# Compressed attention as products on a block diagonal, with the second half's inputs loaded into main attention

## What is computed

```python
def nsa_attend(q, q_pos, kc, vc, ...):
    dist_c = q_pos[:, None] - (jnp.arange(n_cmp) * CMP_STRIDE + (CMP_LEN - 1))[None, :]
    s_c = jnp.einsum('bqghd,bngd->bghqn', q, kc) * SCALE
    s_c = s_c + rb[rel_bucket(dist_c)].transpose(2, 3, 0, 1)
    p_c = masked_softmax(s_c, dist_c >= 0)
    o_c = jnp.einsum('bghqn,bngd->bqghd', p_c, vc)
    ...
    o = gates[:, :, 0][..., None] * o_c + gates[:, :, 1][..., None] * o_s + gates[:, :, 2][..., None] * o_w
```

## Time and profile before

| what | us |
|---|---|
| median of 3 runs | 2063.82 |
| range of the runs | 2063.62 to 2071.12 |
| profiled execution, its own time | 2058.45 |
| span of that execution | 2056.7 |
| TensorE busy | 1857.6 |
| VectorE busy | 1006.2 |
| ScalarE busy | 733.1 |
| GpSimd busy | 542.6 |

### The profile page before, as it was taken

How to read it: one execution, slowest core, us unless ns; L and a number is a source line. 1 busy time by engine, 2 the same in 40 slices (tenths; PEclk the granted TensorE clock), 3 DMA queues, 4 the chain that set the end, 5 groups by cost and what they waited for, 6 DMA issues and landing times. The chain is left out here.

```text
span 2056.7 us, 31665 instructions
## 1 busy us (share of the span) xinstructions
PE 1857.6 (90%) x11624; PEld 1628.5 (79%) x11624; DVE 1006.2 (49%) x1899; ACT 733.1 (36%) x1456; POOL 542.6 (26%) x626
## 2 busy tenths in 40 slices
PE   2988999998877889999998798999999999799995
PEld 2888877997644778778777686999999999776674
DVE  2323421333333557777777652333323232466997
ACT  2223411212322157777777431211111111133352
POOL 4310022421453422222211201112211221143452
PEclk9899999999998579999999899999999999899998
DMA  6452343356987943322221122111111111164533
GB/s 148 87 113 108 133 157 122 115 165 204 315 260 231 229 135 75 66 62 62 63 51 58 75 82 71 42 41 46 55 42 41 43 55 54 37 217 141 189 130 134
DMA packets 168965, 229.21 MB, mean 111 GB/s; under 512 B 44716, under 2 KB 113125, under 8 KB 168711
## 3 DMA queue, kind: packets, MB, share of 16 engines
q1 hardware_dynamic: 144282, 154.58, 25.0%
q0 software_dynamic: 24560, 73.03, 12.8%
HBM read 192.59 MB, written 40.18 MB: 113 GB/s over the span
## 5 line engine op out<-in xcount | busy, mean ns | idle before, releaser
L121 PE MATMUL gate_acc<-o_T_hi,w_gate_split_hi 128*128 128x352 f32 x528 | 171.6, 325 | 2.3 <-ACTq L2696 2.3
L121 PE MATMUL up_acc<-o_T_hi,w_up_split_hi 128*128 128x352 f32 x528 | 170.4, 323 | 0.7 <-DVEq L2739 0.7
L122 PE MATMUL gate_acc<-o_T_lo,w_gate_split_hi 128*128 128x352 f32 x528 | 170.3, 323 | 0.0
L123 PE MATMUL gate_acc<-o_T_hi,w_gate_split_lo 128*128 128x352 f32 x528 | 170.2, 322 | 0.0
L122 PE MATMUL up_acc<-o_T_lo,w_up_split_hi 128*128 128x352 f32 x528 | 169.2, 321 | 0.0
L123 PE MATMUL up_acc<-o_T_hi,w_up_split_lo 128*128 128x352 f32 x528 | 169.1, 320 | 0.0
L2324 DVE TENSOR_TENSOR pa_probs_T_lo<-pa_t,pa_probs_T_hi 128x512 fp32r<-128x512 f32 (+3 forms) x288 | 145.6, 528 | 38.6 <-ACT pa_probs_T_hi L2253 37.3
L2177 PE MATMUL pa_t<-ident,pa_scores 128*128 128x128 f32 x816 | 138.5, 275 | 24.8 <-DVE pa_probs_T_lo L2324 23.9
L2253 ACT ACTIVATE pa_probs_T_hi<-pa_t 128x512 fp32r<-128x512 f32 (+3 forms) x288 | 130.9, 473 | 80.1 <-PE pa_t L2177 74.5
L2238 ACT ACTIVATE pa_scores<-pa_scores,pa_neg_max 128x128 f32<-128x128 f32 (+1 forms) x192 | 143.5, 747 | 16.2 <-DVE pa_neg_max L2276 12.6
L121 PE MATMUL y_acc<-w_down_split_hi,act_split_hi 128*128 128x512 f32 x308 | 125.4, 407 | 19.0 <-DVE act_split_lo L3061 19.0
(11 more groups left out here) (441 smaller groups left out, 4765.5 us busy)
## 6 DMA issues: line engine op xcount, KB each, us to landing
w_down_raw<-in_w_down SPq DMA_DIRECT2D x59, 512.0 KB, 4.3
fox_k_pages<-in_cache_fox_kv SPq DMA_DIRECT2D x64, 256.0 KB, 6.3
w_rows<-in_cache_fox_kv POOLq DMA_DIRECT2D x48, 256.0 KB, 8.1
w_gate<-in_w_gu SPq DMA_DIRECT2D x22, 512.0 KB, 3.7
w_up<-in_w_gu SPq DMA_DIRECT2D x22, 512.0 KB, 3.7
w_rows<-in_w_in SPq DMA_DIRECT2D x5, 2048.0 KB, 10.5
sel_pages<-in_cache_nsa_kv POOLq DMA_DIRECT2D x64, 128.0 KB, 7.5
pa_k_fox<-scratch_kf_d POOLq DMA_DIRECT2D x32, 256.0 KB, 6.3
```

The source lines that it names most:

```text
L121: pe.matmul(out, a[0][at], b[0][bt], start=start, stop=False)
L122: pe.matmul(out, a[0][at], b[1][bt], start=False, stop=False)
L123: return pe.matmul(out, a[1][at], b[0][bt], start=False, stop=stop)
```

## The change

`compressed_attention` computes both key groups in one product. `kc_p` becomes 128 by 128 with each group's 63 keys on the diagonal and zeros elsewhere, and `vc_p` 128 by 136 likewise, with a column of ones for each group, so that the sum of the exponentials comes out of the value product. A tile is 4 score products, 4 turns and 4 value products, each over 128 rows. The turned probabilities are double-buffered in PSUM. VectorE's sum over the exponentials goes; the mask is multiplied into the gates once. `front` zeroes the two tiles on POOL, and `sample_attention` fills them with four copies in place of two.

POOL issues the first half's 16 loads before its fills, splits the fox values of the first half, then issues the second half's 16. SP issues the first half's six loads (the group values go straight into the upper half of the tile that they are split in), waits until the first half's keys have landed, and issues the second half's six. The other five splits are POOL's first work in main attention after its fills. SP's 4 MB copy in main attention waits until the first job is scored. The queries are loaded in two halves of the positions.

```diff
@@ front
-            pool.wait_ge(s_id, 9)
+            pool.memset(c.kc_p[:, :], 0.0).then_inc(s_id, 1)
+            pool.memset(c.vc_p[:, :], 0.0).then_inc(s_id, 1)
+            pool.wait_ge(s_id, 11)
+            for g in range(G):
+                pool.memset(c.vc_p[g * HD:g * HD + NC, P + g:P + g + 1], 1.0).then_inc(s_id, 1)
+            pool.wait_ge(s_id, 13)
@@ sample_attention, SP
-            for g in range(G):
-                sp.dma_start(c.ca_q[g * HD:(g + 1) * HD, :, :], d["qn_d"][g * GH:(g + 1) * GH, :, :].rearrange("h e n -> e h n")).then_inc(c.s_cq, 16)
+            for half in range(2):
+                cols = slice(half * T // 2, (half + 1) * T // 2)
+                for g in range(G):
+                    sp.dma_start(c.ca_q[g * HD:(g + 1) * HD, :, cols],
+                                 d["qn_d"][g * GH:(g + 1) * GH, :, cols].rearrange("h e n -> e h n")).then_inc(c.s_cq[half], 16)
@@ sample_attention, VectorE
-            dve.tensor_copy(c.kc_p[:, :], M[:, 0:NC])
-            dve.tensor_copy(c.vc_p[:, :], M[0:NC, HD:HD + P]).then_inc(s_pv, 1)
+            for g in range(G):
+                rows, cols = slice(g * HD, g * HD + NC), slice(g * HD, (g + 1) * HD)
+                dve.tensor_copy(c.kc_p[cols, rows], M[cols, 0:NC])
+                ins = dve.tensor_copy(c.vc_p[rows, cols], M[rows, HD:2 * HD])
+            ins.then_inc(s_pv, 1)
@@ compressed_attention, SP
             for u in range(2):
+                if u:
+                    sp.wait_ge(pa.s_kl[0], 16 * 8)
+                    settled(sp, c)
                 pa.load_fox_bias(sp, d, GH * u, u)
                 pa.load_fox_values(sp, d, GH * u, u)
-            for n, (kind, u) in enumerate(group):
-                if n >= 2:
-                    sp.wait_ge(pa.s_gs, n - 1)
-                src = d["nsa_kv_p"][0, 0, :, 3, u, :] if kind == "sel" else d["vw_d"][:, u * HD:(u + 1) * HD]
-                sp.dma_start(g_raw[n % 2][:, :, :], src.rearrange("(t p) e -> p t e", p=P)).then_inc(pa.s_gv[n], 16)
-            for u in range(2):
                 pa.load_nsa_bias(sp, d, GH * u, u)
+                for n, (kind, w_) in enumerate(group):
+                    if w_ == u:
+                        src = d["nsa_kv_p"][0, 0, :, 3, u, :] if kind == "sel" else d["vw_d"][:, u * HD:(u + 1) * HD]
+                        sp.dma_start(pa.low_half(kind, u), src.rearrange("(t p) e -> p t e", p=P)).then_inc(pa.s_gv[n], 16)
@@ compressed_attention, POOL (load(u) issues the 16 loads of half u)
+            load(0)
             for u in range(2):
...
-                pool.wait_ge(pa.s_fv[u], 16)
-                pa.split_values(pool, pa.v["fox"][u], pa.v_raw[u], pa.s_vs[u], u + 1)
-            for n, (kind, u) in enumerate(group):
-                pool.wait_ge(pa.s_gv[n], 16)
-                pa.split_values(pool, pa.v[kind][u], g_raw[n % 2], pa.s_gs, n + 3)
+            pool.wait_ge(pa.s_fv[0], 16)
+            pa.split_values(pool, pa.v["fox"][0], pa.v_raw[0], pa.s_vs[0], 1)
+            load(1)
@@ compressed_attention, TensorE: scores, turn, values
                 for m in range(GH):
-                    for g in range(G):
-                        rows = slice(g * HD, (g + 1) * HD)
-                        ins = pe.matmul(S[t % 2][:, g, m * NC:(m + 1) * NC], q[rows, m, t * P:(t + 1) * P], c.kc_p[rows, :],
-                                        start=True, stop=True)
+                    ins = pe.matmul(S[t % 2][:, m, :], q[:, m, t * P:(t + 1) * P], c.kc_p[:, :], start=True, stop=True)
...
-                for h in range(H):
-                    ins = pe.transpose(T_[0:NC, h, :], sc[t % 2][:, h, :], c.ident[:, :])
+                for m in range(GH):
+                    ins = pe.transpose(T_[t % 2][:, m, :], sc[t % 2][:, G * m:G * m + G, :].rearrange("p g n -> p (g n)"), c.ident[:, :])
...
-                for h in range(H):
-                    g = h // GH
-                    ins = pe.matmul(O[t % 2][:, h, :], pT[t % 2][:, h, :], c.vc_p[:, g * HD:(g + 1) * HD], start=True, stop=True)
+                for m in range(GH):
+                    ins = pe.matmul(O[t % 2][:, m, 0:P + G], pT[t % 2][:, m, :], c.vc_p[:, 0:P + G], start=True, stop=True)
@@ compressed_attention, VectorE
-            def coefficients(t):
-                cf = co[:, t, :]
-                dve.wait_ge(s_e, t + 1)
-                chain(dve.tensor_reduce(cf, sc[t % 2][:, :, :], AX, ALU.add))
...
             def output(t):
-                dve.wait_ge(s_co, t + 1)
+                cf = co[:, t, :].rearrange("p (m g) -> p m g", g=G)
                 dve.wait_ge(s_o, t + 1)
+                chain(dve.reciprocal(cf, O[t % 2][:, :, P:P + G]))
+                chain(dve.tensor_tensor(cf, cf, by_pair(gs[:, t, :]), ALU.mult))
@@ prompt_attention, SP
+            sp.wait_ge(s_s, NT + 1)
+            settled(sp, c)
             sp.dma_start(d["win_kv_s"][0, :, 0:WIN - NQ], d["state_win_kv"][0, :, NQ:WIN]).then_inc(s_wc, 16)
@@ prompt_attention, POOL, after its fills
+            for n, (kind, u) in enumerate((kind, u) for u in range(2) for kind in ("sel", "win")):
+                pool.wait_ge(pa.s_gv[n], 16)
+                pa.split_values(pool, v[kind][u], pa.low_half(kind, u), pa.s_gs, n + 2)
+            pool.wait_ge(pa.s_fv[1], 16)
+            pa.split_values(pool, v["fox"][1], pa.v_raw[1], pa.s_vs[1], 6)
@@ prompt_attention, TensorE, values of a sel job
-                        pe.wait_ge(pa.s_gs, 4)
+                        pe.wait_ge(pa.s_gs, 2 * u + 2)
```

More of the change, by code:

```diff
@@ L1765, in __init__ @@
         self.k = {kind: [[ph.sb(f"pa_k_{kind}{u}{w_}", [P, T], FR) for w_ in range(2)] for u in range(2)] for kind in kinds}
+        at_v = ph.nc.sbuf_base
         self.v = {kind: [ph.sb(f"pa_v_{kind}{u}", [P, NT, 2, HD], FR) for u in range(2)] for kind in kinds}
+        assert ph.nc.sbuf_base == at_v + 6 * 2 * NT * HD * 4
+        self.raw = {kind: [ph.nc.alloc_sbuf_tensor_at(f"pa_v_{kind}_raw{u}", [P, NT, 2, HD], F32, offset=at_v + (2 * n + u) * 2 * NT * HD * 4)
+                           for u in range(2)] for n, kind in enumerate(kinds) if n}
         self.v_raw = [ph.sb(f"pa_v_raw{u}", [P, NT, HD]) for u in range(2)]
@@ L1818, in compressed_attention @@
         q = c.ca_q
-        sc = [ph.sb(f"ca_scores{i}", [P, H, NC]) for i in range(2)]
-        pT = [ph.sb(f"ca_probs_T{i}", [NC, H, P]) for i in range(2)]
-        g_raw = [ph.sb(f"pa_group_v_raw{n}", [P, NT, HD]) for n in range(2)]
+        sc = [ph.sb(f"ca_scores{i}", [P, H, HD]) for i in range(2)]
+        pT = [ph.sb(f"ca_probs_T{i}", [P, GH, P]) for i in range(2)]
         mx = ph.sb("ca_max", [P, 2, H])
+        gs = ph.sb("ca_gates", [P, NT, H])
         co = ph.sb("ca_coef", [P, NT, H])
-        S = [ph.ps(f"ca_s{i}", [P, G, 512]) for i in range(2)]
-        T_ = ph.ps("ca_t", [P, H, P])
-        O = [ph.ps(f"ca_o{i}", [P, H, HD]) for i in range(2)]
+        S = [ph.ps(f"ca_s{i}", [P, GH, P]) for i in range(2)]
+        T_ = [ph.ps(f"ca_t{i}", [P, GH, P]) for i in range(2)]
+        O = [ph.ps(f"ca_o{i}", [P, GH, 256]) for i in range(2)]
         s_s = ph.sem("ca_scored")
+        s_z = ph.sem("ca_cleared")
         s_sh = ph.sem("ca_shifted")
@@ L1856, in _, with load @@
         def _(pool):
[L1857 to L1861, removed]
+            def load(u):
                 pa.load_fox(pool, d, GH * u, u)
@@ L1867, in _ @@
                             pool.dma_start(pa.k[kind][u][w_][r * HD:(r + 1) * HD, :], d[src][w_, u]).then_inc(pa.s_kl[u], 16)
+            load(0)
             for u in range(2):
-                pool.wait_ge(pa.s_fv[u], 16)
-                pa.split_values(pool, pa.v["fox"][u], pa.v_raw[u], pa.s_vs[u], u + 1)
-            for n, (kind, u) in enumerate(group):
-                pool.wait_ge(pa.s_gv[n], 16)
-                pa.split_values(pool, pa.v[kind][u], g_raw[n % 2], pa.s_gs, n + 3)
+                pool.memset(pa.bias["sel"][u][:, 0:T - 256], 0.0).then_inc(pa.s_bz, 1)
+                pool.memset(pa.bias["win"][u][:, P:WIN + P - 256], 0.0)
+                pool.tensor_copy(pa.bias["win"][u][:, 0:P], misc(c, "wmask", P)).then_inc(pa.s_bz, 1)
+            pool.wait_ge(pa.s_fv[0], 16)
+            pa.split_values(pool, pa.v["fox"][0], pa.v_raw[0], pa.s_vs[0], 1)
+            load(1)
         @block.tensor
@@ L1877, in scores @@
             def scores(t):
[L1878 to L1879 removed]
+                if t % (NT // 2) == 0:
+                    pe.wait_ge(c.s_cq[t // (NT // 2)], 16 * G)
                 if t >= 2:
@@ L1930, in _ @@
             chain = Chain(dve, s_ch)
-            chain.enter(0, NT * 5)
+            chain.enter(0, 3 + NT * 4)
             lo = MISC["seen"][0]
+            by_pair = lambda y: y.rearrange("p (g m) -> p m g", g=G)
+            chain(dve.tensor_tensor(gs[:, :, :], c.gates[:, 0:NT, 0:H], c.misc[:, lo:lo + NT * H].rearrange("p (t h) -> p t h", h=H), ALU.mult))
+            for x in sc:
+                chain(dve.memset(x[:, :, NC:HD], 0.0))
             def shifted(t):
```

(10 more changed lines are left out.)

36 lines of the change are left out of this document (15 added, 21 removed).

## The result

The changed kernel takes 2055.13 us (median of 5 runs, 2051.48 to 2060.25); the kernel before, run beside it, took 2063.82 (2060.8 to 2072.01). The ratio is 0.995 with a 95% interval of 0.9926 to 0.9973: faster by 6 to 15 us, where 18.4 were forecast, and outside the range of 2032 to 2052. The profiled execution took 2058.64 us, its span is 2056.9.

The account below looks back on a forecast made before the run. TensorE at the lower clock was taken to bound compressed attention, SP's held issues to end it after the change. 18.7 us saved less 0.3 for copies gave 18.4: 2045.4 us from the 2063.82 median, range 2032 to 2052.

Parts of the forecast that it names:

- Rival (d): Compressed attention, TensorE: wide f32 passes don't overlap weight loads, 0.44 us each, 14 us slower, 2078 us; chance 5%.
- The rule on weight loads: TensorE: a weight load overlaps a running matmul only when the row group differs, true of nothing after the change.
- The queries in halves and the small fills: Ahead of the stage: about 1.7 us more on SP and 1 us on POOL, both expected to hide in waits.
- (a): Compressed attention: SP isn't held by a full queue, computation ends the stage; 2032 us, or 2044 at lower clock; chance 18%.
- (c): Main attention gives the gain back through late POOL merges or second-half values, 10 us or more; 2054 to 2064; chance 9%.
- Rival (b): Compressed attention ends later, at 724 to 730, by 0.26 us passes or a slower queue; 2047 to 2054 us; chance 8%.
- the sum of the part on the transfers: Compressed attention: SP's last issue ends at 720.8, main attention starts at 721.5 in place of 740.26, 18.7 us less.
- The rate of POOL's packets: Compressed attention: POOL's and SP's queues move 69 packets a us each, one for one; POOL's is through at 718.4.
- The end of the block: End of compressed attention: main attention starts 0.74 us after SP's last issue, the last of the engines' work.
- The room in SP's queue: Compressed attention: SP's queue holds 2300 to 2600 packets, so its last issue ends with 4310 to 4610 of 6912 done.

Follow-up runs that it names:

- the transfers alone: The kernel before with only the change's transfers and value splits, the old narrow products kept: 2065.21 us, ratio 0.9997 to the kernel before.

## Why the prediction was wrong

**Right.** TensorE bound the stage at the lower clock and does so no longer; the wide passes cost 0.235 and 0.11 us; the upper clock came, and the computation ended 29.6 us after the start against 30.8 forecast. Rival (d) is out: a pass of 0.235 us, not 0.44. The rule on weight loads that the prediction names beside it, from the Trainium skill ("TensorE: Matmul & The Clock Gate", Part 3, The mechanism), does not hold for these passes. The stage ends on transfers with TensorE idle, and an issue of SP of many us stands before it. POOL's splits and the delayed copy, both moved behind the stage, cost nothing that shows: the rest after the stage is 1316.7 against 1316.4. The queries in halves and the small fills lie ahead of a stage whose start varies by 13 us, so these profiles can't show their microsecond. Rivals (a) and (c) are out as well. Rival (b), to which I gave 8%, is what happened: it had a slower queue and the stage's end at 724 to 730, and 677.2 + 50.2 is 727.4. Its 2047 to 2054 still ends 1 us under the median of the result.

**The step that failed** is the sum of the part on the transfers, which took SP's last issue plus 0.74 us for the end of the stage. The stage ended on another path, POOL's packets and the DRAIN behind them, and these packets were slower than forecast. The sum let main attention start 44.3 us after the stage did; it was 50.2. All its counts can be held against the DMA queues of the changed kernel (windows 694.15 to 702, 702 to 715.2, and 715.2 to 737.1, then SP's from the start to 731.6, to 735.8 and to 737.5; packets, MB, share):

```profile
q0 software_dynamic: 368, 1.24, 74.8%
q1 hardware_dynamic: 1117, 0.48, 51.9%
...
q0 software_dynamic: 947, 3.10, 95.3%
...
q0 software_dynamic: 1243, 4.04, 78.5%
q1 hardware_dynamic: 2426, 1.22, 53.3%
...
q1 hardware_dynamic: 3601, 1.79, 45.7%
...
q1 hardware_dynamic: 4249, 2.24, 48.2%
...
q1 hardware_dynamic: 5231, 2.65, 50.7%
```

1. *The rate of POOL's packets* is the term that made the time. I took 69 a us, from the middle of the stage before, for the whole of it, and one packet of SP for one of POOL's. It was 368/7.85 = 47 in the first 8 us, where SP's queue moved three packets for one of POOL's, 947/13.2 = 72 then, and 1243/21.9 = 57 for the second half, with a slow tail: 236 packets in the last 6.8 us, beside 1252 of SP's. POOL's queue was through 46.7 us after the start, not 41.2. The earlier start of POOL, on which I counted, bought little: its 1280th packet began 24.7 us after the start of the stage in the changed kernel and 25.3 in the kernel before, whose first had come 2.8 us later.
2. *The end of the block.* I took 0.74 us behind SP's last issue, which is right when VectorE or SP is last, and never asked for POOL beyond its last issue. POOL's packets ended at 736.79, its DRAIN at 739.16, and main attention began at 740.24, 3.45 us behind the packets. SP alone (737.50 and 1.0) would have given 738.5.
3. *The room in SP's queue.* I had 2300 to 2600 packets from two issues. Each of SP's loads also has 16 packets of 4 B, which I had left out: 3552 a half and 7104 in all, not 3456 and 6912. The long issue was let go when 3601 of the 4736 packets issued before it had begun (3593 in the kernel without the wait), so with about 1130 left; SP's last issue ended with 5231 of 7104 begun, so with 1870 left. SP's queue had begun 4249 by 735.8, and would by the forecast's room have let SP go just behind, at about 736; it went on to 737.50. So SP was free 47.5 us after the start, not 43.6. By itself this set nothing, since POOL's DRAIN ended 1.4 us after SP's.

The account of the 5.9 us is then: POOL's packets were through 5.5 us later than forecast, and the way from there to main attention (3.45 us) is 0.35 longer than the 3.1 that the forecast had from POOL's last packet, by way of SP, to the same point. It was luck that the missing wait was so small a term: by the forecast's own rate POOL's queue ends at 41.2, and with 3.45 main attention begins at 44.6, beside the 44.3 of the sum. As a mechanism it is what the prediction lacked. It holds the stage at 44.6 us when SP has no second half to issue, and of the 19 us between the changed kernel's stage and that of the best version, 17.6 go when POOL's second half alone goes, 5.6 when SP's alone does.

From 44.3 to 50.2 in the stage the sum would have been 2051.3. The medians of the changed kernel (2055.13 and 2053.11) lie 2 to 4 us above that; that gap is within the scatter of single runs, and no run says more about it. Why sample attention takes 179 to 193 us from one execution to the next stays open as well.

**A version that beats both.** Both second halves in main attention: 2033.33 us, ratio 0.9833 (0.9797 to 0.9869), 22 us under the changed kernel (24 by the ratios). Its stage ends on the computation, 30.4 us after the start. The risk of rival (c), that main attention pays for it, is answered by its 1316.2 us behind the stage.

## What to carry to other kernels

Before a stage's computation is made faster, ask of POOL's queue when its last packet lands, not only when its last issue ends, and look at how long POOL's DRAIN at the end of a block takes. For SP the last issue counts. A load that the next stage wants late belongs into the next stage, on both queues: there it cost nothing, here 19 us. A packet rate read in the middle of a stage isn't that of its first 8 us, where other packets share the engines, nor of its tail.

## What the runs showed of the hardware

- A block's end waits for the packets that POOL has issued, not for SP's: the same 4 MB copy made a stage 46.9 us long when POOL issued it and 30.4 when SP did. What waits is POOL's DRAIN: it ended 1.3 to 2.4 us behind the last packet of POOL's queue in nine kernels, where SP's took 0.007 us with its own packets on the way. With POOL last, the barrier opened 2.0 to 3.5 us after its last packet or operation; with VectorE or SP last, 0.7 to 1.1 us.
- An issue of SP with 128 packets was held for 13.21 us behind 2000 others, and took 0.58 us in the same place with POOL's second half gone and 1180 others before it. Held issues were let go with 1130 to 1350 packets still waiting (3601 begun of 4736 issued; 2204 of 3552), the last one ended with 1870, so the room isn't one fixed number, and the 2300 to 2600 of the prediction were too many.
- In the nine kernels with 128-row, 128-column passes TensorE was at the lower clock, 1.2 GHz, for the first 3 to 9 us of the stage and at the upper, 2.4 GHz, from there to the end of the computation. In the three with the narrow passes (the kernel before, its repeat, and the transfers alone) it stayed at 0.50 for all 63 us, though it was busy for 58 of them. So the upper clock came with the new computation and not with the new transfers.
